# Order of the first loads and of the modulation steps in a fused two-layer diffusion block

## What is computed

```python
ml = jnp.split((c_act @ w_mod[i] + b_mod[i])[:, None, :], 6, axis=-1)      # the same with cc_act for the context
hl = modulate(xl, norm_mix_g[i], ml[0], ml[1])       # rms_norm(x, g) * (1 + scale) + shift
xl = xl + ml[2] * yl
xl = xl + ml[5] * squared_relu_mlp(modulate(xl, norm_mlp_g[i], ml[3], ml[4]), w_mlp_in[i], w_mlp_out[i])
```

## Time and profile before

| | |
|---|---|
| median of 3 executions | 1681.24 us (1681.19 to 1683.17) |
| the profiled execution | 1683.28 us, span 1681.5 us, so 1.78 us lie around the span |
| TensorE busy | 97% of the span |
| VectorE, ScalarE, GpSimd busy | 53%, 31%, 37% |
| head, up to the first weight matmul | 46.79 us |
| MLP of layer 0 | from about 390 to 948 us |

### The profile page before, as it was taken

The page is one execution under the profiler, slowest core; times in us unless marked ns, Lnnn a source line. Parts: engine busy times, 40 slices in busy tenths (PEclk is TensorE's granted clock), DMA queues, the critical chain, the costliest instruction groups (busy, mean ns, idle before and its releaser), DMA issues.

```text
span 1681.5 us, 23855 instructions
## 1 busy us (share of the span) xinstructions
PE 1627.6 (97%) x9350; PEld 1366.2 (81%) x9350; DVE 885.2 (53%) x1173; ACT 521.4 (31%) x928; POOL 616.3 (37%) x395
## 2 busy tenths in 40 slices
PE   5899989999899999999999999999999999999997
PEld 2777878888788888888888888877857988888887
DVE  2400207627862772684486667319964753535264
ACT  3422327524211211121122421128853522222122
POOL 1422246324432332332332343344502644444441
PEclk7999999999999999999999999999999999999999
DMA  9364121311342342323243032200001232222221
GB/s 366 135 255 153 63 66 55 120 57 64 101 174 66 99 150 101 100 100 137 77 137 100 27 109 79 77 24 2 4 37 63 78 111 92 97 99 100 88 88 51
DMA packets 50636, 163.97 MB, mean 98 GB/s; under 512 B 6504, under 2 KB 8808, under 8 KB 46960
## 3 DMA queue, kind: packets, MB, share of 16 engines
q1 hardware_dynamic: 50544, 162.68, 27.9%
HBM read 159.77 MB, written 2.10 MB: 96 GB/s over the span
## 4 chain that ended last, share of the span: by engine, by line
PE 92%; DVE 3%; issue 1%; ACT 1%; DMA 1%; POOL 1%; SPq 0%; POOLq 0%; DVEq 0%; ACTq 0%
PE ps L1513 26%; PE ps L1514 26%; PE ps L1515 26%; PE ps L1964 2%; PE ps L1926 2%; PE ps L1953 1%; PE ps L1834 1%; PE ps L1824 1%; PE ps L1708 1%; PE ps L1862 1%; DMA xc<-ctx_dram 1%; PE ps L1857 1%; PE ps L1720 0%; PE ps L2020 0%; PE ps L1975 0%
## 5 line engine op out<-in xcount | busy, mean ns | idle before, releaser
L551 POOL TENSOR_TENSOR w_lo<-raw,w_hi 128x1024 fp32r<-128x1024 f32 (+1 forms) x228 | 482.7, 2127 | 916.6 <-ACT w_hi L704 916.6
L1513 PE MATMUL ps<-h,w_hi 128*128 128x512 f32 (+1 forms) x1176 | 413.9, 352 | 5.4 <-DVE h L1170 4.4
L1514 PE MATMUL ps<-h,w_lo 128*128 128x512 f32 (+1 forms) x1176 | 412.0, 350 | 0.0
L1515 PE MATMUL ps<-h,w_hi 128*128 128x512 f32 (+1 forms) x1176 | 409.6, 348 | 0.0
L704 ACT ACTIVATE w_hi<-raw 128x1024 fp32r<-128x1024 f32 x189 | 199.7, 1057 | 402.2 <-PE ps L1515 395.7
L1513 PE MATMUL ps<-hid_lo,w_hi 128*128 128x512 f32 (+1 forms) x800 | 279.3, 349 | 0.0
L1514 PE MATMUL ps<-hid_hi,w_lo 128*128 128x512 f32 (+1 forms) x800 | 278.8, 349 | 0.0
L1515 PE MATMUL ps<-hid_hi,w_hi 128*128 128x512 f32 (+1 forms) x800 | 277.2, 347 | 0.0
L1513 PEld LDWEIGHTS ps<-h,w_hi 128*128 128x128 f32 x1176 | 223.2, 190 | 44.7 <-issue 11.2
L1515 PEld LDWEIGHTS ps<-h,w_hi 128*128 128x128 f32 x1176 | 222.3, 189 | 30.3
L1514 PEld LDWEIGHTS ps<-h,w_lo 128*128 128x128 f32 x1176 | 223.2, 190 | 28.4
(11 more groups left out here) (206 smaller groups left out, 2185.0 us busy)
## 6 DMA issues: line engine op xcount, KB each, us to landing
raw<-units_dram SPq DMA_DIRECT2D x189, 512.0 KB, 3.3
mod_ring<-w_mod_dram SPq DMA_DIRECT2D x96, 256.0 KB, 3.1
mod_big<-w_mod_dram SPq DMA_DIRECT2D x16, 1024.0 KB, 8.7
mod_late<-w_mod_dram SPq DMA_DIRECT2D x8, 1024.0 KB, 6.4
xl<-x_dram SPq DMA_DIRECT2D x2, 2048.0 KB, 11.6
bias<-bias_dram SPq DMA_DIRECT2D x8, 384.0 KB, 3.8
xc<-ctx_dram SPq DMA_DIRECT2D x2, 1024.0 KB, 13.6
out_dram<-out_t SPq DMA_DIRECT2D x16, 128.0 KB, 1.9
```

Of the source, the lines that this page charges most:

```text
L551: ins = nc.gpsimd.tensor_tensor(w_lo[:, s, sl], raw[:, s, sl], w_hi[:, s, sl].bitcast(F32), op=ALU.subtract)
L1513: mm(out, a[0], b[1], start=start, stop=False)
L1514: mm(out, a[1], b[0], start=False, stop=False)
L1515: return mm(out, a[0], b[0], start=False, stop=stop)
```

## The change

In the head, the conditioning vector gets a semaphore of its own and is loaded first, followed at once by chunks 0 and 1 of the modulation, then three constants, `x` and `ctx`, the other three constants, chunk 2. Weight units 0 to 2 are issued when the first half of chunk 3 has landed, unit 3 when its second half has. The work on `lam` moves on each engine from ahead of the modulation to behind its first two chunks, where VectorE first waits for the six other constants. ScalarE's square-root table is asked for ahead of the squares. TensorE turns chunk 2 ahead of multiplying chunk 3, and turns chunk 3 ahead of spreading the norm's factors. ScalarE rounds the first weight units behind chunk 3's copy. The scales are computed one chunk at a time. GpSimd's first three low parts are made in four pieces each. In the MLP of layer 0, chunks j = 1 and 2 are summed during output units 8 to 11 and not 4, 5, 8 and 9, and `mod_mm` comes after units 5, 10 and 12 and not 4, 8 and 12.

```diff
-MOD_AT = {4 * j: (j, range(0, 4)) for j in range(3)}
-MOD_AT |= {4 * j + 1: (j, range(4, 8)) for j in range(3)}
-MOD_TURN = {4: 0, 8: 1, 12: 2}
+MOD_AT = {i: (j, range(0, 4)) for j, i in enumerate((0, 8, 10))}
+MOD_AT |= {i: (j, range(4, 8)) for j, i in enumerate((1, 9, 11))}
+MOD_TURN = {5: 0, 10: 1, 12: 2}
...
@@ sync
-            for dst, name in ((cond, "cond"), (ident, "ident"), (b_mod, "b_mod"), (gains, "gains"),
-                              (mask, "mask"), (lam_in, "lam"), (subg, "subln")):
-                sp.dma_start(dst[:], t[name]).then_inc(consts_in, 16)
...
-            for m in range(4):
-                if m == 3:
-                    sp.wait_ge(half_summed, 1)
-                load_half_mod(m)
-                if m == 1:
-                    sp.dma_start(xl[:], t["x"]).then_inc(x_in, 16)
-                    sp.dma_start(xc[:], t["ctx"]).then_inc(x_in, 16)
+            sp.dma_start(cond[:], t["cond"]).then_inc(cond_in, 16)
+            load_half_mod(0)
+            load_half_mod(1)
+            for dst, name in ((ident, "ident"), (lam_in, "lam"), (b_mod, "b_mod")):
+                sp.dma_start(dst[:], t[name]).then_inc(consts_in, 16)
+            sp.dma_start(xl[:], t["x"]).then_inc(x_in, 16)
+            sp.dma_start(xc[:], t["ctx"]).then_inc(x_in, 16)
+            for dst, name in ((gains, "gains"), (mask, "mask"), (subg, "subln")):
+                sp.dma_start(dst[:], t[name]).then_inc(consts_in, 16)
+            load_half_mod(2)
+            sp.wait_ge(half_summed, 1)
+            load_half_mod(3)
...
-            for u in range(SLOTS):
+            sp.wait_ge(big_in[0][0], mod_slot(3)[1])
+            for u in range(AHEAD):
                 load_unit(u, u, True)
+            sp.wait_ge(big_in[0][1], mod_slot(3)[1])
+            load_unit(AHEAD, AHEAD, True)
+            sp.wait_ge(raw_in[AHEAD - 1], 16)
@@ gpsimd
             for u in range(AHEAD):
-                low(u, u)
+                low(u, u, 4)
@@ scalar
-            act.wait_ge(consts_in, 16 * 7)
+            act.wait_ge(cond_in, 16)
             nc.scalar.activation(ctmp[:], cond[:], ACT.Exp, scale=-1.0).then_inc(exp_c, 1)
-
-            act.wait_ge(lam_mm, 1)
-            nc.scalar.activation(lam_t[:, 2:4], ps[:, 6, 0:2], ACT.Exp).then_inc(lam_exp, 1)
...
             half_rows(0)
             half_rows(1)
+            act.wait_ge(lam_mm, 1)
+            nc.scalar.activation(lam_t[:, 2:4], ps[:, 6, 0:2], ACT.Exp).then_inc(lam_exp, 1)
+            act.wait_ge(ones_ok, 1)
+            nc.scalar.activation(stat[:, 63:64], eps_c[:, 0:1], ACT.Sqrt)
             act.wait_ge(x_in, 32)
...
             norm_root(0, 1)
+            half_rows(3)
             high_u(0)
             high_u(1)
-            half_rows(3)
             high_u(2)
@@ vector
-            def scales(i):
+            def scales(i, halves=(0, 1)):
...
+                for a in halves:
+                    dve.wait_ge(mod_done, m + a + 1 if i < 2 else 24)
+                    st.wait(V.scalar_tensor_tensor(out=gs[:, i, 0:vs, 4 * a:4 * a + 4], in0=mods[:, m + a, 0:vs, :], scalar=1.0,
+                                                   in1=gains[:, i, 4 * a:4 * a + 4].unsqueeze(1).broadcast_to([P, vs, 4]),
+                                                   op0=ALU.add, op1=ALU.mult))
...
             V.tensor_copy(cact_wide[:, :, 0:2], cact[:]).then_inc(cact_ok, 1)
+            dve.wait_ge(consts_in, 16 * 6)
+            lam = lam_in[:].rearrange("p (a b) -> p a b", b=2)
+            tt(lam_t[0:HD, 0:2], lam[:, :, 0], lam[:, :, 1], op=ALU.mult).then_inc(lam_ok, 1)
...
             half_add(0)
+            dve.wait_ge(lam_exp, 1)
...
             half_add(2)
+            scales(0, (0,))
             half_add(3)
-            scales(0)
+            scales(0, (1,))
@@ tensor
                         if layer == 0 and i in MOD_TURN:
-                            if first and i == 4:
-                                pe.wait_ge(relu_made, ha(0, 0, 3))
                             mod_mm(b, MOD_TURN[i])
...
-            pe.wait_ge(ones_ok, 1)
-            pe.wait_ge(lam_ok, 1)
-            mm(ps[:, 6, 0:2], ones[0:HD, :], lam_t[0:HD, 0:2], start=True, stop=True).then_inc(lam_mm, 1)
...
             half_mm(0)
             half_mm(1)
+            pe.wait_ge(ones_ok, 1)
+            pe.wait_ge(lam_ok, 1)
+            mm(ps[:, 6, 0:2], ones[0:HD, :], lam_t[0:HD, 0:2], start=True, stop=True).then_inc(lam_mm, 1)
             half_turn(0)
             half_mm(2)
             half_turn(1)
+            pe.wait_ge(lam_exp, 1)
             norm_sums(0, 0)
             norm_sums(0, 1)
+            half_turn(2)
             half_mm(3)
+            half_turn(3)
             norm_spread(0, 0)
             norm_spread(0, 1)
-            half_turn(2)
-            half_turn(3)
```

More of the change, by code:

```diff
@@ L245, in sem @@
             return ctx.enter_context(nc.semaphore(name))
+        cond_in = sem("cond_in")
         consts_in = sem("consts_in")
@@ L1103, in extract @@
                 ins.then_inc(mod_done, 1)
-            def scales(i):
+            def scales(i, halves=(0, 1)):
                 m = 12 * (i // 2) + 2 * (1 + 3 * (i % 2))
[L1108 to L1113, removed]
-                st.wait(ins)
+                vs = 2 if i < 3 else 1
+                for a in halves:
[3 more added lines that the diff above has]
+                                                   op0=ALU.add, op1=ALU.mult))
             def sum_squares(i, m):
@@ L1313, in _ @@
             dve.sem_inc(ones_ok, 1)
-            dve.wait_ge(consts_in, 16 * 7)
-            lam = lam_in[:].rearrange("p (a b) -> p a b", b=2)
-            tt(lam_t[0:HD, 0:2], lam[:, :, 0], lam[:, :, 1], op=ALU.mult).then_inc(lam_ok, 1)
             dve.wait_ge(exp_c, 1)
@@ L1321, in _ @@
             V.tensor_copy(cact_wide[:, :, 0:2], cact[:]).then_inc(cact_ok, 1)
+            dve.wait_ge(consts_in, 16 * 6)
+            lam = lam_in[:].rearrange("p (a b) -> p a b", b=2)
+            tt(lam_t[0:HD, 0:2], lam[:, :, 0], lam[:, :, 1], op=ALU.mult).then_inc(lam_ok, 1)
             V.tensor_reduce(group_sum[:], ident[:].rearrange("p (g v) -> p v g", g=4)[:, 0:2], AX.X, ALU.add).then_inc(group_ok, 1)
             V.tensor_scalar(subg[:, 1:2], subg[:, 0:1], 1.0 - LAM_INIT, None, ALU.mult)
-            dve.wait_ge(lam_exp, 1)
-            st.wait(V.scalar_tensor_tensor(out=lam_t[:, 4:5], in0=lam_t[:, 3:4], scalar=LAM_INIT,
-                                           in1=lam_t[:, 2:3], op0=ALU.subtract, op1=ALU.subtract))
             def half_add(m):
@@ L1334, in _ @@
             half_add(0)
+            dve.wait_ge(lam_exp, 1)
+            st.wait(V.scalar_tensor_tensor(out=lam_t[:, 4:5], in0=lam_t[:, 3:4], scalar=LAM_INIT,
+                                           in1=lam_t[:, 2:3], op0=ALU.subtract, op1=ALU.subtract))
             for k in range(6):
```

## The result

| | before | after |
|---|---|---|
| median of 14 executions each | 1681.43 us (1681.19 to 1683.17) | 1684.61 us (1683.42 to 1690.35) |
| ratio | | 1.0019, 95% interval 1.0011 to 1.0028 |
| the profiled execution | 1683.28 us, span 1681.5 | 1683.48 us, span 1681.7 |
| first weight matmul | 46.79 us | 47.71 us |

The change costs 0.19%, 3.2 us by the medians, and that lies just within the 0.2% (3.4 us) that the forecast called no change: the forecast of no change holds by 0.2 us, and the interval reaches past 0.2%. Against the forecast of 1681.9 us the median is 2.7 us higher, inside the range of 1676.5 to 1686.0. Both halves of this have to be read: where the time went in the profiled pair, and why the typical execution after is slower than the profiled one.

The account below looks back on a forecast made before the run. TensorE was taken as the bound nearly everywhere, so only its idle and lower-clock time could change. Terms -6.8 + 0.7 + 3.25 + 2.0 + 1.5 = +0.65 took the median from 1681.24 to 1681.9 us, range 1676.5 to 1686.0.

Parts of the forecast that it names:

- Term A: MLP of layer 0, first block: TensorE's 4.77 us wait at `mod_mm` and 2.04 lost at half clock go; -6.8 us.
- Term B: MLP of layer 0, seven of eight turns of chunks 1 and 2: 0.1 us each; +0.7, bounds 0 to 2.1.
- term C: Last MLP block's `mod_mm` in `tail`: the sum comes 8.5 us after unit 11, TensorE after 5.25; wait of +3.25 us.
- Term D: Behind the new wait in `tail`: time lost at half clock, between 0 and 2.85 us, taken as +2.0.
- Term E: Head: squares later, first weight matmul 0.8 to 2.4 us later, partly repaid by the clock; +1.5, bounds -1.2 to 4.2.
- the low clock level carries on: Rival, head and behind `tail`'s wait: low clock lasts longer, head and tail together over 9.5; +3.8, 1685.0 us; chance 0.18.
- The late waits do not open: Rival, MLP tail and turns: C 1.4, B 0, D 0, head costs 0.3; -5.1, 1676.1 us; chance 0.24.
- The six constants do not land behind `ctx`: Rival, head: squares begin at 21.8, head gains 3.1 against term E; -2.4, 1678.8 us; chance 0.07.

Follow-up runs that it names:

- the kernel before with the sums apart: Kernel before, own head, chunk 1 summed at units 6 and 7, chunk 2 at 9 and 10, first `mod_mm` wait left out: 1676.41 us, ratio 0.9962.
- with the sums apart: Kernel after with chunk 1 summed at units 6 and 7, chunk 2 at 9 and 10, `mod_mm` after 5, 9, 12: 1678.47 us, ratio 0.9984.
- the kernel before with the new tables: Kernel before with only the MLP part of the change, `mod_mm` after units 5, 10, 12, and without the first block's explicit wait: 1682.40 us, ratio 0.9997.
- the useless matmuls: Kernel after with fourteen useless matmuls ahead of the last `mod_mm` in `tail`, into a bank overwritten later: 1681.97 us, ratio 1.0003.
- The head alone: Kernel after with the MLP's old summing places, `mod_mm` after units 4, 8, 12, and the old wait: 1684.16 us, ratio 1.0010.
- with the table late: Kernel after without the early square root, so its table is loaded where the norm's first root needs it: 1684.14 us, ratio 1.0022.

## Why the prediction was right, and where it was off

**Term A (-6.8), the first block's wait: right.** The milestones show -6.9, and the same gain stands alone in the kernel before with the sums apart (-5.3 by the medians, -6.6 between like executions).

**Term B (+0.7), the seven turns: too small by half.** The profiled pair shows +1.5, and the kernel before with the new tables the same steps. The two turns of the first block cost nothing, the other five 0.26 to 0.38 each. The pattern was copied rightly: in the last block the split ends 8.37 after unit 9 is seen, to the hundredth. The step that failed is the choice of 0.1 a turn. I took off a square sum that most turns do not have, and left out the 0.15 of the hop that I counted in term C. Without square sums the first row starts at 620.24, 0.01 behind GpSimd's subtraction (620.23), and is blocked for 2.93, longer than the 2.62 of the pattern. The split then ends at 627.41, 0.16 before VectorE sees unit 10 done at 627.57, and TensorE's weight load for the turn waits 0.23. The turns of chunk 2, which have `extract` ahead of their rows, cost hardly more (0.28 and 0.29) than those of chunk 1, which have none (0.27 and 0.26 in the same blocks); even the addition of 128x4 blocked for 2.20 (row 904.49, 0.16 when free) leaves VectorE idle 0.35 before unit 11 is seen. The term is within the bounds of 0 to 2.1.

**Term C (+3.25), the tail: right.** The wait is 3.44, with one row blocked for 2.56 and the matmul 8.9 after unit 11 was seen, for 8.5 forecast.

**Term D (+2.0), the clock behind it: right.** 1.9 by milestones, 1.75 by the windows; and the useless matmuls, which take only the idleness away, bring back 1.6 by milestones and 2.6, with an uncertainty of about 1, by the medians.

**Term E (+1.5), the head: right in its chain, too small in the typical execution.** Each link came as described: `subg` landed behind `ctx`, the `lam` matmul at 22.83 (22 to 23 forecast), the table load directly before the squares, the squares at 25.01 (24.9), the second k-step's wait at 0.81 (0.6). For the table load the trace shows 1.28 and the ACTIVATE 0.01 behind it: the row was right, no drain is to be seen. The Trainium skill ("ScalarE: Activation LUTs", What ACT_TABLE_LOAD costs), with its drain, would have put the squares 1.4 later; the trace does not agree.

What the sum mis-sized is the clock, on both sides of the first weight matmul. Ahead of it I gave 0.8 to 2.4 late and took a value in the middle; the profiled execution shows 0.9, three other profiles of the same head show 2.1 to 2.2, the slow end. Both ends of the working came out: 11.2 to 12.8 us from the sums to the matmul were forecast, 11.1 and 12.5 measured. Behind it, I took the 2.85 lost at half speed, and half of any delay paid by it, from one execution, and wrote that no term depends on its lying 2.04 over the median. Term E does: with the same head, the run with the MLP part alone loses 1.5 there, and reaches the MLP 1.9 earlier. So the head after begins to differ from a typical execution before by more than the profiled pair shows. At the first rectification in the MLP the three other profiles with the head after stand 1.0 to 1.5 behind the profiled execution of before, and 2.9 to 3.4 behind that run; the kernel after stands 0.3 and 2.2 behind them. That the executions of before near 1681.4 and those near 1683.2 are these two heads fits their distance, but each is seen in one or two profiles only.

The head alone costs 2.2 by its own experiment, and by the medians of the whole, 3.2 less what the MLP part adds (0.4), 2.8. That is half-way to the head of the rival "the low clock level carries on" (3.8). The rival's own sign, head and tail together over 9.5, is not met: 2.8 + 3.4 + 1.9 = 8.1. Its other half, a longer stretch behind `tail`, did not come, and that rival's total, 1685.0, is nearer to the median than the forecast is. The shortfalls of E (1.3, with E at 2.8) and B (0.8) are 2.1 of the 2.7 us by which the forecast was low; the remaining 0.6 I cannot place. In the profiled pair the sum looks better than it is: +0.2 measured for +0.65, because E came out 1.2 too high there and B 0.8 too low. That is luck, and so is the 0.2 us by which the median stays inside 0.2%.

**The other rivals.** "The late waits do not open" is ruled out by the wait of 3.44. "The six constants do not land behind `ctx`" is ruled out by the releaser of VectorE's 19.03 us; what it would have brought was then seen by moving them: squares at 21.87 and 2.4 us.

So "no change" was the balance of two real effects. The removed wait was worth 6.9, and 5.3 of it went into a wait of the same kind some 475 us later; the earlier load was worth 2.6 and went into three constants and a table load, and the new order behind the sums cost up to 1.6 more.

## What to carry to other kernels

When work on a side engine is moved to close one wait of TensorE, write down its distance to the consumer at every place it recurs, the last short iteration above all: here one unit's distance in `tail` took back 5.3 of the 6.9 us won. Here a small transfer behind large ones on the same queue landed 15 us after its issue, so a wait for "all constants" must not count any that is issued behind the big loads. And in this MLP TensorE's idles of 3.4 and 4.8 us each cost about 2 us more for the clock behind them; filling the one with useless matmuls gave 1.6 of that back. Last, a profiled execution that lies 2 us over the median is not a neutral base for a sum: ask in which stage it lost them.

## What the runs showed of the hardware that I had not expected

The length of a stretch at the lower clock is not fixed by the instructions in it. In the head of before, with the first weight matmul at 46.8 to 46.9 each time, the clock was back at full at 52.5 in one profile and at 49.8 in another. At the start of layer 1's output projection, with the same waits ahead, it was at half for 3.4, 6.8, 10.2 and 20.5 us in six profiles (6.8 in three of them), and the kernels differ only in what stands hundreds of us earlier. Executions of one kernel fall in groups 5 to 6 us apart (1678.0 to 1678.9 and near 1683.9 with the sums apart; 1681.6 to 1684.4 and near 1690 with the table late). That these groups are a short and a long stretch fits the sizes, but it is inferred: only one execution of each kernel was profiled. A difference of 5 us between two variants of this kernel is therefore not yet a difference between their codes, and it takes the distribution, or the windows of the clock, to tell.
